# Router product turned round: weights stationary, tokens in two halves; three expert loads held back in the second layer

## The reference, cut to what matters

```python
x = layer_norm(DEEPNORM_ALPHA * x + m, ln1_g[i], ln1_b[i])
f = hier_moe(x, router_wg[i], router_bg[i], router_we[i], router_be[i], exp_w1[i], exp_w3[i], exp_w2[i])

def hier_moe(x, wg, bg, we, be, w1, w3, w2):      # 512 tokens, 64 experts in 8 groups
    g_logits = xt @ wg + bg                        # 8 values a token
    e_logits = (xt @ we + be)[group of the token]  # 8 of 64 values a token
    g_top = argmax(g_logits); e_val, e_loc = top_k(e_logits, 2)
    gate = softmax(e_val) * softmax(g_logits)[g_top]
    # every token goes through its two experts, h = silu(x @ w1[e]) * (x @ w3[e]), y = h @ w2[e],
    # and its two results are added, each times its gate
```

## Time and profile before

| what | value |
|---|---|
| median of 3 runs | 3114.56 us (3110.7 to 3115.47) |
| the profiled execution, its own time | 3118.68 us |
| its span in the profile | 3116.3 us |
| TensorE busy | 2908.4 us (93%) |
| mean granted clock of TensorE | 0.964 |
| expert loads (the page's list of DMA issues) | 1024.0 KB each, 28 us from issue to landing in the middle |
| first expert layer, from the router's transposes to the last expert matmul | 1686 to 2201 us |
| second expert layer, the same | 2564 to 3081 us |

### The profile page before, as it was taken

One profiled execution on the slowest core, in us unless ns is written; L12 is line 12 of the kernel. 1 busy time (PEld: TensorE's weight loads), 2 busy tenths in 40 slices (PEclk: granted clock), 3 DMA queues, 4 the chain that ended last, 5 costly groups with the idle time before them and its releaser, 6 DMA issues.

```text
span 3116.3 us, 43193 instructions
## 1 busy us (share of the span) xinstructions
PE 2908.4 (93%) x17806; PEld 2269.3 (73%) x17806; DVE 1474.1 (47%) x2611; ACT 948.1 (30%) x1782; POOL 576.7 (19%) x500
## 2 busy tenths in 40 slices
PE   8999999999999999999999898888699998998885
PEld 7659999998888788888887555555577775555553
DVE  5635423353444563233745453333588854543334
ACT  4543413233223434142422121111335721211112
POOL 1402201110111212021000442222000003522220
PEclk9999999999999999999998999999899997999997
DMA  4012232222222223233236899999622238999996
GB/s 143 21 62 69 95 94 83 95 79 79 78 85 73 72 73 108 82 99 104 82 106 236 338 414 415 417 416 416 225 82 70 71 130 340 412 414 417 416 416 268
DMA packets 239099, 599.28 MB, mean 192 GB/s; under 512 B 32617, under 2 KB 177508, under 8 KB 189742
## 3 DMA queue, kind: packets, MB, share of 16 engines
q1 hardware_dynamic: 214500, 568.43, 48.0%
q0 software_dynamic: 23904, 27.90, 2.8%
q10 hardware_dynamic: 490, 0.08, 0.0%
HBM read 606.69 MB, written 39.89 MB: 207 GB/s over the span
## 4 chain that ended last, share of the span: by engine, by line
PE 82%; DVE 6%; DMA 4%; issue 3%; ACT 2%; SPq 1%; POOL 0%; ACTq 0%; DVEq 0%; POOLq 0%
PE ps L101 77%; PE ps L104 5%; DMA sb_ring<-in_exp_w_dram 3%; DVE sb_arena L126 1%; SPq L144 1%; DVE sb_ws L118 1%; DVE sb_tmpA L118 1%; DVE sb_arena L118 1%; DVE sb_tmpA L126 1%; DVE sb_hT L126 0%; ACT sb_ws L112 0%; DVE sb_hT L118 0%; ACT sb_arena L112 0%; DMA sb_arena<-y_rows 0%; DVE sb_hs L126 0%
## 5 line engine op out<-in xcount | busy, mean ns | idle before, releaser
L101 PE MATMUL ps<-sb_hs,sb_ws 128*128 128x264 f32 (+1 forms) x5856 | 1009.7, 334 | 9.7 <-DVE sb_ws L118 4.5
L101 PEld LDWEIGHTS ps<-sb_hs,sb_ws 128*128 128x128 f32 x5856 | 886.4, 189 | 128.1 <-DVE sb_ws L118 9.8
L118 DVE TENSOR_TENSOR sb_ws<-sb_ring,sb_ws 128x1024 fp32r<-128x1024 f32 x279 | 365.2, 1312 | 438.0 <-ACT sb_ws L112 437.6
L112 ACT CAST sb_ws<-sb_ring 128x1024 fp32r<-128x1024 f32 x279 | 290.8, 1045 | 376.2 <-PE ps L101 360.6
L101 PE MATMUL ps<-sb_arena 128*64 128x256 f32 (+18 forms) x1652 | 348.3, 417 | 23.3 <-issue 16.4
L101 PE MATMUL ps<-sb_br,sb_ws 128*128 128x264 f32 (+1 forms) x2304 | 367.4, 322 | 0.0
L101 PEld LDWEIGHTS ps<-sb_br,sb_ws 128*128 128x128 f32 x2304 | 332.5, 188 | 34.1 <-issue 0.5
L101 PE MATMUL ps<-sb_ring,sb_arena 128*64 128x256 f32 (+2 forms) x1506 | 284.8, 445 | 34.9 <-issue 32.2
L108 ACT ACTIVATE sb_arena<-ps 64x256 f32<-64x256 f32 (+6 forms) x192 | 76.0, 407 | 731.1 <-PE ps L101 706.5
L118 DVE TENSOR_TENSOR sb_arena<-sb_arena,ps 64x256 f32<-64x256 f32 (+1 forms) x160 | 66.3, 423 | 485.1 <-ACT sb_arena L108 451.2
L101 PEld LDWEIGHTS ps<-sb_arena 128*64 128x64 f32 (+6 forms) x1652 | 198.0, 159 | 123.7 <-issue 65.7
(11 more groups left out here) (218 smaller groups left out, 2873.7 us busy)
## 6 DMA issues: line engine op xcount, KB each, us to landing
sb_ring<-in_exp_w_dram SPq DMA_DIRECT2D x113, 1024.0 KB, 28.4
sb_hx<-in_exp_w_dram SPq DMA_DIRECT2D x92, 1024.0 KB, 28.2
sb_arena<-in_exp_w_dram SPq DMA_DIRECT2D x66, 1024.0 KB, 28.1
sb_wx<-in_exp_w_dram SPq DMA_DIRECT2D x66, 1024.0 KB, 28.0
sb_ring<-in_mlp_w_dram SPq DMA_DIRECT2D x64, 1024.0 KB, 5.3
sb_hT<-in_exp_w_dram SPq DMA_DIRECT2D x47, 1024.0 KB, 28.2
sb_ring<-in_od_w_in_dram SPq DMA_DIRECT2D x24, 1024.0 KB, 5.2
sb_ring<-in_conv_w_in_dram SPq DMA_DIRECT2D x12, 1024.0 KB, 5.1
```

Source lines behind the costliest of these rows:

```text
L101: return self.e.matmul(o, l, r, start=start, stop=stop, skip_group_check=True)
L112: return self.e.copy(o, i)
L118: return self.e.tensor_tensor(o, a, b, op)
```

## The change

1. The transposes of X no longer fill units slice by slice. `raw_rows_pe` puts tokens 0 to 255 into two units and tokens 256 to 511 into the other two. `raw_rows_act` and `raw_rows_dve` copy each half as four pieces of 128x512 (two slices of 256 tokens), two by each engine. The transposes no longer wait for the router's weights; `route_pe` still does.
2. Order on the engines: ScalarE copies both halves and then centres tile 1. VectorE copies the first half, takes the reciprocals, copies the second half, and then centres tiles 0, 2 and 3.
3. The router's product: for each half eight matmuls with the weights (128x72) stationary and 256 tokens moving. The result is 72x256; ScalarE copies it to SBUF (`logits_half`), and TensorE turns it back in two transposes. Those of the first half are issued behind the second matmul of the second half. `route_dve` reads the turned logits.
4. Places 12 and 13 wait for the last router matmul, as before under a new key. In the second layer, load 14 (and 15 and 16 behind it) also waits until the first gathered rows have landed.
5. Two scratch rows are moved.

```diff
-            turn_pe(e, units, (l, 0))
+            raw_rows_pe(e, units, l)

+        def raw_rows_pe(e, units, l):
+            key = (l, 0)
+            us = [units.take(e, ("bank", key, i)) for i in range(4)]
+            emptied(e, ("turn", l, 7))
+            for t in range(4):
+                for f in range(8):
+                    at = 256 * (f % 4) + 128 * (t % 2)
+                    q = e.tp(us[2 * (t // 2) + f // 4][:, at:at + 128],
+                             X[:, t, :].rearrange("s (h p o) -> s h o p", h=2, o=4)[:, f // 4, f % 4, :], ident)
+                    if f % 2:
+                        q.then_inc(*turned.mark(("x", key, t, f)))
+        def raw_rows_act(e, l, h):
+            for p in (1, 3):
+                e.wait_ge(*turned["x", (l, 0), 2 * h + 1, 2 * p + 1])
+                e.acp(*raw_pair(l, h, p)).then_inc(
+                    *act_emptied.mark(("bank", (l, 0), 2 * h + p // 2), ("raw x", l, h, p)))
+        def raw_rows_dve(e, l, h):
+            for p in (0, 2):
...
         def finish_act(e, l):
             for t in range(4):
                 rs_act(e, t, (l, 0))
-            for t in range(4):
-                centre_act(e, t, (l, 0))
-            turn_act(e, (l, 0), False)
+            raw_rows_act(e, l, 0)
+            raw_rows_act(e, l, 1)
+            centre_act(e, 1, (l, 0))

         def finish_dve(e, l):
             for t in range(4):
                 bn(e, t, 3)
                 mean_dve(e, t, (l, 0))
+            raw_rows_dve(e, l, 0)
             for t in range(4):
                 root_dve(e, t, (l, 0))
             router_shift_dve(e, l)
-            for t in (0, 2):
+            raw_rows_dve(e, l, 1)
+            for t in (0, 2, 3):
                 centre_dve(e, t, (l, 0))
-            turn_dve(e, (l, 0), False)
-            centre_dve(e, 3, (l, 0))
...
             elif i in (12, 13):
-                e.wait_ge(*summed[("r", (l, 0)), 3])
+                e.wait_ge(*summed["logits", l, 1])
...
             for n in range(EARLY[l], PLACES):
+                if (l, n) == (1, PLACES - 3):
+                    e.wait_ge(*xg_in[0][l, 0])
                 moe_load(e, l, n)
...
+        def logits_turned_pe(e, units, l, h):
+            u = units.take(e, ("turned logits", l, h))
+            emptied(e, ("logits", l, h))
+            for i in range(2):
+                q = e.tp(u[:, 128 * i:128 * i + 72], logits_half(h)[:, 128 * i:128 * i + 128], ident[0:72, 0:72])
+            q.then_inc(*turned.mark(("logits", l, h)))

         def route_pe(e, units, l):
             e.wait_ge(*dve_route["router", l])
-            tok_pe(e, units, ("r", (l, 0)), 72, ("router", l))
+            v, us = router_view(l), []
+            for h in range(2):
+                us.append(units.take(e, ("logits", l, h)))
+                for k in range(8):
+                    if h and k == 2:
+                        logits_turned_pe(e, units, l, 0)
+                    if k % 2 == 0:
+                        emptied(e, ("raw x", l, h, k // 2))
+                    q = e.mm(us[h][0:72, 0:256], v[:, k, :], xT(k, 0)[:, 256 * h:256 * h + 256], k == 0, k == 7)
+                q.then_inc(*summed.mark(("logits", l, h), *([("router", l)] if h else [])))
+            logits_turned_pe(e, units, l, 1)
...
         def moe_act(e, l):
+            for h in range(2):
+                e.wait_ge(*summed["logits", l, h])
+                e.acp(logits_half(h), U_["logits", l, h][0:72, 0:256]).then_inc(*act_emptied.mark(("logits", l, h)))
...
-                    e.wait_ge(*summed[key, t])
+                    e.wait_ge(*turned["logits", l, t // 2])
```

More of the change, by code:

```diff
@@ L2054, in turn_pe @@
             us = [units.take(e, ("bank", key, i)) for i in range(4)]
-            if key[1] == 0:
-                emptied(e, ("turn", key[0], 7))
-                e.wait_ge(*dve_route["router", key[0]])
             for t in range(4):
-                if key[1]:
-                    e.wait_ge(*centred(key, t))
+                e.wait_ge(*centred(key, t))
                 for f in range(8):
@@ L2111, in load_gb, with raw_pair @@
             e.dma(GB[:, 1, :], spread(A[GROWS[2 * kind + 1]], 1024 * l, 1024)).then_inc(*gb_in.land(key))
+        def raw_rows_pe(e, units, l):
[9 more added lines that the diff above has]
+                        q.then_inc(*turned.mark(("x", key, t, f)))
+        def raw_pair(l, h, p):
+            dst = grid(WX[:, 1024 * p + 256 * h:1024 * p + 256 * h + 1], (512, 2), (1, 256))
+            return dst, U_["bank", (l, 0), 2 * h + p // 2][:, 512 * (p % 2):512 * (p % 2) + 512].rearrange(
+                "p (a b) -> p a b", a=2)
+        def raw_rows_act(e, l, h):
[5 more added lines that the diff above has]
+            for p in (0, 2):
+                e.wait_ge(*turned["x", (l, 0), 2 * h + 1, 2 * p + 1])
+                e.cp(*raw_pair(l, h, p)).then_inc(
+                    *dve_emptied.mark(("bank", (l, 0), 2 * h + p // 2), ("raw x", l, h, p)))
         def finish_pe(e, units, l):
-            turn_pe(e, units, (l, 0))
+            raw_rows_pe(e, units, l)
         def finish_act(e, l):
@@ L2891, in route_dve @@
                     G = lg[:, t, 0:8]
-                    e.wait_ge(*summed[key, t])
+                    e.wait_ge(*turned["logits", l, t // 2])
                     e.wait_ge(*step["shift", l])
-                    e.stt(lg[:, t, :], tok_out(key, t, 72), stats(t)[2], router_shift(), ALU.mult, ALU.add).then_inc(
-                        *(dve_emptied.mark((key, t // 2)) if t % 2 else step.mark(("logits", l, t))))
-                    e.wait_ge(*(dve_emptied[key, t // 2] if t % 2 else step["logits", l, t]))
+                    u = U_["turned logits", l, t // 2][:, 128 * (t % 2):128 * (t % 2) + 72]
+                    e.stt(lg[:, t, :], u, stats(t)[2], router_shift(), ALU.mult, ALU.add).then_inc(
+                        *(dve_emptied.mark(("turned logits", l, t // 2)) if t % 2 else step.mark(("logits", l, t))))
+                    e.wait_ge(*(dve_emptied["turned logits", l, t // 2] if t % 2 else step["logits", l, t]))
                     e.e.max(eight(m8g, t), G).then_inc(*step.mark(("g8", l, t)))
```

13 lines of the change are left out of this document (4 added, 9 removed).

## The result

| kernel | median of its runs | profiled execution: span | mean granted clock |
|---|---|---|---|
| before | 3116.16 us (3110.7 to 3122.16, 20 runs) | 3116.3 us | 0.964 |
| changed | 3108.57 us (3105.47 to 3114.17, 20 runs) | 3111.1 us | 0.968 |

The ratio is 0.9975, interval 0.9968 to 0.9981: the changed kernel is faster by 7.6 us of medians (5.9 to 10.0 us by the interval). The forecast was a gain of 9.4.

What follows compares the result with a forecast made beforehand. The loads were taken as the bound once TensorE has used up the 17 ahead, so the first expert's time counts. First layer 3.9 plus second 5.5 gives 9.4 us: 3114.56 - 9.4 = 3105.2 us, range 3101.0 to 3112.5.

Steps and rivals of the forecast that it cites:

- The path to the first expert: Both expert layers: a layer ends as much earlier as its first expert is done, microsecond for microsecond; 3.9 and 5.5 us.
- The sign that the loads would go on at full share: Second layer's DMA: loads at full share again from the first `up_mm` on; a new gap there would show the prediction wrong.
- The clock: Router product on TensorE: full clock throughout, 7.1 us for 16 matmuls; the other bound, at half clock, 14.2 us.
- A: Router product: the clock falls as now, second layer gains 0.1, first nil, gather 2.9 remains; 3111.6 us, chance 0.17.
- C: Router product: half clock from the first matmul in both layers, 2.6 to 5.6 us slower, 3117.2 to 3120.2; chance 0.06.
- E: Router transposes: the clock is lost there and returns within the product, which costs 1.5 us; 3106.7 us, chance 0.05.
- rival B: Second layer's row write: no bound, landing before 2587, so that layer gains 7.3, together 11.0; 3103.6 us, chance 0.17.
- VectorE is the bound behind the product: Router selection: VectorE bound from tile 0 on, 8.5 us in the second layer; selection 3.9 and 4.4 us earlier.
- The rows' landing as the next wait: Second layer: lists ready at 2587.0, so the gather waits for GpSimd's row writes, taken to land at 2588.5.
- The quiet gather: Second layer's first gather: with three loads held it meets idle queues and takes 2.6 instead of 5.5 us.
- rival D: Second layer's second gather lands late: central case but 3 us less gain, 3108.2 us, chance 0.13.
- First layer: First layer's router: selection over at 1703.8 against 1707.73, a gain of 3.9 us.

Runs made afterwards that it cites:

- the hold: The wait of the second layer's loads 14 to 16 for the first gathered rows; the changed kernel without it: 3112.34 us, ratio 0.9990.
- five held: The changed kernel with five loads (12 to 16) of the second layer waiting for the first gathered rows instead of three: 3105.86 us, ratio 0.9971.
- the combination: Changed kernel with the product's old form fed by halves, centring before second-half copies, GpSimd's clearing before its row writes, three loads held: 3103.78 us, ratio 0.9963.
- the 16 transposes in the gap: Changed kernel, product held back until VectorE has centred tile 0, the wait filled with 16 unused identity transposes: 3108.12 us, one execution.
- the run with the gap: Changed kernel with the product waiting until VectorE has centred tile 0, about 2.1 us of idle: 3112.37 us, ratio 0.9988.
- the combination with five held: Changed kernel with old-form product fed by halves, earlier centring, clearing before the row writes, and five loads held instead of three: 3105.22 us, ratio 0.9966.
- the old form fed by halves: Changed kernel with 32 matmuls of 72 moving columns, no way back through ScalarE, transposes and copies by halves: 3108.70 us, ratio 0.9979.

## Why the prediction was right, and where it was off

The sum and the result: 3116.16 - 9.4 = 3106.8 would have been the forecast against this median of before; 3108.57 came. Point by point:

1. **The path to the first expert sets the end.** Held in sign, not fully in size. What the first expert wins comes out at the layer's end by 3.74 of 3.94 us in the first layer, 2.98 of 3.77 in the second, 2.4 of 5.1 for the hold (2.8 of 5.6 in the old order), 2.3 of 4.1 for five held. So "microsecond for microsecond" was too much. Wherever the gain was bought with idle DMA engines, part of it was given back; that this is because the loads are the bound behind the first expert is argued, not shown. And each figure is a difference of two single executions, which spread: three executions with the changed kernel's first layer unaltered and "up" at T+33.9 to 34.0 have "last" at T+509.15, 511.08 and 511.33, and in the combination's second layer 2.3 us of the first expert left nothing. The sign that the loads would go on at full share from the first `up_mm` on was missed by the 0.9 us shown above.
2. **The clock.** Right, and shown twice over: product 7.2 us (7.1 forecast), clock 1.00 to its end, in both layers of every execution without a gap. The rivals A, C and E fall. (Two readings in the prediction are off by 0.1: the clock rose at 2229.2, since that window's clock is 0.89 and 0.93 is its busy time, and rival B's terms add to 10.9. Neither matters.) E had the Trainium skill's rule for it (TensorE: Matmul & The Clock Gate, Part 4: PE-mode transpose: transposes don't count as busy). By that rule the 16 transposes in the gap should have done nothing; they kept the clock at 1.00 through 6 us of transposes and the product behind them, so this trace speaks against the rule for float32 transposes of 128x128, as the rise at 2229 did, behind transposes alone. That the fall was *sure* before was wrong: 2 of 6 routers of the old order kept their clock. In the second layer this matters little, for the gather then waits for the rows and flies through the load traffic; in the first layer all three profiled executions of the old order fell.
3. **VectorE is the bound behind the product.** Right, better than forecast: selection 4.51 and 4.74 us earlier (3.9 and 4.4). No word was said of GpSimd's clearing, which held a VectorE operation for 0.4 to 0.7 us in both kernels.
4. **The rows' landing as the next wait.** Right as a wait; rival B falls. **Its size is the term that failed.** The prediction put the landing at T+24.9 ("I take 2588.5 for the landing"), 0.4 us behind the end of the traffic at T+24.5. The traffic did end at T+24.7 (2585.0), but the last row landed at about T+26.5, 18.4 us after its issue, and the gather went out at T+27.41 against T+25.8. That is 1.6 us, and it is nearly the whole difference between 5.5 and 3.77 at the second layer's first expert. The prediction saw that the first three writes would go out 2.4 us later, but charged nothing for it, since the fourth kept its time. The runs say that it counts: with the first writes at T+3.95 (old order, with the hold and without it) the gather was released at T+25.50 and 25.56, with all four from T+5.11 on at T+25.5 and 26.6, from T+6.30 on at T+27.3 to 28.2. The reason can be seen in the four landings, which come one behind the other, 3.7 to 4.5 us apart: T+13.0, 17.4, 21.1 and 24.8 before, T+14.7, 18.4, 22.2 and 26.5 changed. Counted from the first write's issue the last landing took 20.9 and 20.2 us, nearly the same; the 17.0 us that the prediction carried over held for the fourth write behind earlier ones. One execution spreads: in the run with the gap the last row landed at T+25.5 from the same issues, so the size is known to about 1 us.
5. **The quiet gather.** Right: 2.6 us in place of 5.5; the second gather took 2.5 us too, so rival D falls.
6. **First layer.** 3.94 us against 3.9, by two errors that cancel: the selection gained 0.6 more, and the first `up_mm` took 6.22 us where it had taken 5.7, because the clock came back later. The repeated run of the same kernel had 4.56 there ("up" at T+33.93), so this is a spread of single executions.

**Why the spans differ by 5.2 only.** The layers' own lengths, T to "last" of both layers added, are 1032.93 us before and 1026.21 after, 6.7 less, and in the repeated profiles 1033.61 and 1025.60, 8.0 less. The other 1.5 us of the first pair lie in code that the change doesn't touch: 1.1 behind the second layer's last expert (35.04 and 36.17 us to the end), 0.4 between the layers. The start of the first router spreads as much: T is 1682.5 to 1684.2 in seven of the executions and 1685.3 to 1686.3 in the other seven, whatever the kernel. The windows show where, long before any changed line. The kernel before:

```profile
100.00:200.00 100.00, 89.65 (x383) 0.95 0.17 53
200.00:300.00 100.00, 100.00 (x694) 0.98 0.14 43
```

and the combination with five held (T 1682.71):

```profile
100.00:200.00 100.00, 89.64 (x388) 0.97 0.17 53
200.00:300.00 100.00, 100.00 (x713) 1.00 0.14 43
```

In the late executions the granted clock is low for longer in the first 300 us. In all seven late executions these two windows have 0.95 and 0.98, in all seven early ones 0.97 and 1.00, and 1 to 4 us lie between the two groups at T. Two profiles of two versions must be compared from a common mark on, not by their spans.

## What to carry to other kernels

When a product runs at half clock, look at what TensorE did in the microseconds before it, not at the product: closing a gap of 1.75 us took 5.5 us off the product, and reshaping it took off 0.1. At the end of the kernel that was worth about 4 us over two layers, by the run with the gap put back. Where a gap can't be closed, it can be filled with work whose result is thrown away, if that is over when the operands arrive (one execution shows it). When a wait on DMA moves onto the path, take its landing from a row under the same load; where several writes land one behind the other, count from the issue of the first of them and not of the last, and move that issue; and an idle DMA queue, bought to make one small transfer fast, has to be paid for where the loads are the bound.

## What the runs showed of the hardware that was not expected

- A VectorE operation (TENSOR_SCALAR, 128x8, one input tensor and a per-partition scalar, all in SBUF) that meets a GpSimd MEMSET of 1.8 us ends with it: 0.87 and 0.63 us before, 0.91 changed, 2.11 in the old form fed by halves (it had even begun 0.25 us before the MEMSET), 0.22 to 0.23 with the MEMSET out of the way. The MAX8, FIND_INDEX8 and CAST just ahead of it ran beside the same MEMSET at their usual 0.15 to 0.17 us. The Trainium skill (GPSIMD Engine Reference, 8. Key points) says that GpSimd shares its SBUF interfaces with VectorE and gets in the way of VectorE's instructions in a 2-port mode or with two SBUF inputs; which of the two this operation is, no trace here says.
- The last row's landing under a full load queue came 18.4 us after its issue, and 1.8 us after the DMA engines had gone quiet (share 0.07).
- Of two executions of one kernel, one lost the clock in its second router and the other kept it; with the gap and the product turned round it was lost and came back after 3.4 us, while in the old order it stayed down to the end of the product.
- At full clock a float32 matmul with 72 columns moving took 7.32/32 = 0.229 us, 3.2 ns a column, and one with 256 moving 7.20/16 = 0.45 us, 1.76 ns a column. The product needs 32 of the first and 16 of the second, so it takes nearly the same time in both forms; why a column costs more in the first, no run here says.
